# Two-layer decoder step: router products on column strips, the expert gather ahead of row numbers and weights, modulation pages moved, pages in pairs, pooling in parts

## The reference, cut to what matters

```
mod = silu(c) @ w_ada + b_ada            # 6 vectors of 1024: shift, scale, gate for mixer and for ffn
h = rms_norm(x, g_mix) * (1 + sc1) + sh1
q, k, v, u, g = split(h @ w_in)          # 4096 columns: 512, 512, 512, 512, 2 x 1024
o = differential attention(q, k, v)      # samples also read 256 cached keys and values each
y_pool = (trailing mean of u over 2/4/8/16 - u) @ w_pool
x = x + gt1 * ((g0 * (o @ w_branch[:512]) + g1 * (y_pool @ w_branch[512:])) @ w_out)
h2 = rms_norm(x, g_ffn) * (1 + sc2) + sh2
layer 0: f = (silu(h2 @ wg) * (h2 @ wu)) @ wd                       # dense, 2816 wide
layer 1: logits = h2 @ w_router; top 2 of 8 experts, softmax of the two
         f = sum over experts of weight * swiglu(h2, expert)        # each 3584 wide
x = x + gt2 * f
```

## Time and profile before

| what | value |
|---|---|
| median of 3 runs | 1683.52 us (1680.14 to 1684.52) |
| the profiled execution | 1683.85 us, span 1682.2 us |
| busy share of the span | PE 97%, PE weight load 61%, DVE 25%, ACT 9%, POOL 4% |
| DMA | 535.43 MB, mean 318 GB/s |
| chain that ended last | PE 80%, DMA 11%, DVE 4%, SP queue 3% |
| mean granted TensorE clock | 0.985 |

### The profile page before, as it was taken

The page is one execution under the profiler, slowest core; times in us unless marked ns, Lnnn a source line. Parts: engine busy times, 40 slices in busy tenths (PEclk is TensorE's granted clock), DMA queues, the critical chain, the costliest instruction groups (busy, mean ns, idle before and its releaser), DMA issues.

```text
span 1682.2 us, 35169 instructions
## 1 busy us (share of the span) xinstructions
PE 1624.7 (97%) x15778; PEld 1018.8 (61%) x15778; DVE 422.9 (25%) x966; ACT 158.4 (9%) x410; POOL 66.6 (4%) x114
## 2 busy tenths in 40 slices
PE   6999999999999989999999999999999999999997
PEld 3778887888886878882444444444445645445454
DVE  3368343101113784432101010101010101010114
ACT  2102301000002112130100000000000000000000
POOL 3101300000000010001000000000000000000100
PEclk8999999999999999988999999999999999999999
DMA  9999978564439987427999999999999999999995
GB/s 340 365 346 321 293 252 256 152 204 143 147 111 339 300 267 200 136 55 272 397 409 404 401 408 400 407 408 395 403 393 405 403 392 402 405 393 406 407 397 194
DMA packets 275562, 535.43 MB, mean 318 GB/s; under 512 B 17837, under 2 KB 167003, under 8 KB 262610
## 3 DMA queue, kind: packets, MB, share of 16 engines
q1 hardware_dynamic: 259920, 497.12, 81.5%
q0 software_dynamic: 8608, 28.65, 5.0%
q10 hardware_dynamic: 6882, 7.37, 1.4%
HBM read 517.70 MB, written 15.82 MB: 317 GB/s over the span
## 4 chain that ended last, share of the span: by engine, by line
PE 80%; DMA 11%; DVE 4%; SPq 3%; issue 1%; another core or an unknown queue 0%; ACT 0%; DVEq 0%
PE bank L1357 29%; PE bank L1377 13%; PE bank L1050 12%; PE bank L951 9%; PE bank L1247 5%; DMA ring<-in_w_exp_gate 4%; PE bank L1223 3%; DMA ring<-in_w_exp_up 3%; PE bank L1211 2%; PE bank L959 2%; SPq L573 1%; DMA area<-in_w_exp_down 1%; DMA ring<-in_w_ada 1%; DMA area<-q_rows 1%; SPq L590 1%
## 5 line engine op out<-in xcount | busy, mean ns | idle before, releaser
L1357 PE MATMUL bank<-ring,area 128*32 128x448 f32 x3072 | 294.6, 541 | 7.2 <-issue 3.9
L1357 PE MATMUL bank<-ring,xT 128*32 128x448 f32 x3072 | 294.5, 539 | 4.8 <-issue 3.0
L463 DVE TENSOR_TENSOR area<-bank,area 128x224 f32<-128x224 f32 x96 | 54.2, 564 | 787.4 <-ACT area L907 787.3
L1050 PE MATMUL bank<-hT,ring 128*128 128x264 f32 x1024 | 242.2, 392 | 2.2 <-ACT hT L744 2.2
L1357 PEld LDWEIGHTS bank<-ring,area 128*32 128x32 f32 x3072 | 115.6, 110 | 178.6 <-issue 163.8
L1357 PEld LDWEIGHTS bank<-ring,xT 128*32 128x32 f32 x3072 | 115.1, 110 | 176.2 <-issue 167.0
L1377 PE MATMUL bank<-area 128*32 128x256 f32 x3840 | 217.7, 379 | 3.2 <-issue 2.8
L1050 PEld LDWEIGHTS bank<-hT,ring 128*128 128x128 f32 x1024 | 194.4, 192 | 39.9 <-issue 6.7
L1377 PEld LDWEIGHTS bank<-area 128*32 128x32 f32 x3840 | 138.9, 110 | 75.0 <-issue 5.1
L951 PE MATMUL bank<-hT,ring 128*128 128x264 f32 x704 | 157.4, 386 | 0.0
L951 PEld LDWEIGHTS bank<-hT,ring 128*128 128x128 f32 x704 | 133.7, 190 | 23.2 <-issue 0.4
(11 more groups left out here) (296 smaller groups left out, 901.2 us busy)
## 6 DMA issues: line engine op xcount, KB each, us to landing
ring<-in_w_exp_gate SPq DMA_DIRECT2D x256, 448.0 KB, 14.4
ring<-in_w_exp_up SPq DMA_DIRECT2D x256, 448.0 KB, 14.9
area<-in_w_exp_down SPq DMA_DIRECT2D x64, 1024.0 KB
ring<-in_w_ada SPq DMA_DIRECT2D x96, 512.0 KB, 8.4
ring<-in_w_in SPq DMA_DIRECT2D x64, 512.0 KB, 9.3
ring<-in_w_exp_down SPq DMA_DIRECT2D x32, 1024.0 KB, 15.6
area<-in_w_exp_down SPq DMA_DIRECT2D x32, 512.0 KB
ring<-in_w_ff_gate SPq DMA_DIRECT2D x22, 512.0 KB, 6.9
```

Source lines behind the costliest of these rows:

```text
L463: dve.tensor_tensor(F["act_tok"][:, t, :].rearrange("p (i n) -> p n i", i=BODY), bank[t][:, SLICE:2 * SLICE].rearrange("p (n i) -> p n i", ...
L1050: mm = pe.matmul(bank[b][:, 0:T], w[:, c, :], hT[:, c, :], start=(c == 0), stop=(c == DC - 1))
L1357: mm = pe.matmul(bank[t][32 * g:32 * g + 32, 0:2 * SLICE].rearrange("p (s n) -> p s n", s=2), tokens[:, t, 32 * r:32 * r + 32], w[:, :, SL ...
```

## The change

- `later_ada` puts four modulation pages behind every second strip in place of two behind each. In layer 1 only pages 32 to 39 stay there; 40 to 47 go to the end of the stream, behind the output projection, and PE uses them in the router stage (40 to 43 ahead of the rank sums, 44 to 47 behind them). DVE reads them there (`read_mod(1, 7, 40, 47, ...)`, eight pages at a time).
- Strips of the input projection, of `w_branch` and of `w_out` are loaded two by two, one DMA of 1 MB with rows of 1 KB (`PAIRED`, `pair_cols`). SP waits until both slots are free, PE until the pair has landed.
- The sample values are used behind strips 27 and 29, four pages each.
- `pooling()` is split: the windowed sums and group 0 come behind `read_z(13)`, groups 1 to 3 behind `read_z(14)`, and both first `past_scores` behind `read_z(15)`.
- Router: `w_router` is the weight, padded to 32 columns; the eight chunks go to four column strips of PE in two rounds, `hT` moves (264 columns). DVE copies the four partial sums, and three products with a constant `fold` matrix add them and give tokens by experts. The transposes of `hT` stand around these products, chunk by chunk. ACT copies the x tokens between the norm's square root and its shift additions.
- Experts: DVE makes `got` first, then `most`, the modulation read and the three turns of gathered tiles; row numbers and weights follow. `gate_up_turn` waits tile by tile; the routing transposes behind turn 0 wait for a new semaphore `wt_ready`. The gather uses banks 3 to 5.
- Expert pages of turn 0 wait for pairs; the last six of the 16 now wait for modulation pages 40 to 45.
- The zeros tile is half as wide, and the 16 zero stores of layer 0 have rows of 1 KB.

```diff
         def later_ada(l, i):
-            first, last = ((16, 48), (32, 48))[l]
-            return range(first + 2 * i, min(first + 2 * i + 2, last))
+            first, last = ((16, 48), (32, 40))[l]
+            return range(first + 2 * (i - 1), min(first + 2 * (i + 1), last)) if i % 2 else range(0)
...
+            if l:
+                for n in range(40, 48):
+                    yield ada_page(l, n)
...
             for n, (key, src) in enumerate(stream):
+                if key[0] in PAIRED:
+                    if key[2] % 2 == 0:
+                        if n >= RING:
+                            sp.wait_ge(s.pages_used, freed(n + 1 - RING))
+                        sp.dma_start(pair_cols(n % RING), src).then_inc(page_in[n % RING], 16)
+                    continue
...
-                            sp.wait_ge(s.pages_used, STRAIGHT - RING + 2 * r + half + 1)
+                            sp.wait_ge(s.pages_used, STRAIGHT - RING + 2 * r + 2)
...
-                        pooling()
-                    if i >= 14:
-                        past_scores(i - 14)
+                    if i == 13:
+                        window_sums()
+                        pooled_minus_own(0)
+                    if i == 14:
+                        for g in range(1, H):
+                            pooled_minus_own(g)
+                    if i == 15:
+                        past_scores(0)
+                        past_scores(1)
...
+            def route(half):
+                for g in range(4):
+                    c = 4 * half + g
+                    mm = pe.matmul(bank[6][32 * g:32 * g + 32, 0:T], w_route[:, c, :], hT[:, c, :],
+                                   start=(half == 0), stop=(half == 1), skip_group_check=True)
+                if half:
+                    mm.then_inc(s.route_mm, 1)
+            pe.wait_ge(s.tok_out, 6)
+            for c in range(4):
+                pe.wait_ge(s.h_ready, DC * (2 * LAYERS - 1) + c + 1)
+                turn_h(c)
+            route(0)
+            pe.wait_ge(s.h_ready, DC * 2 * LAYERS)
+            route(1)
+            turn_h(4)
+            pe.wait_ge(s.logits_kept, 1)
             for i in range(3):
                 rows = min(P, T - i * P)
+                mm = pe.matmul(bank[6][0:rows, 272 + E * i:272 + E * i + E], FFN["wt_wide"][:, i * P:i * P + rows], const("fold"),
+                               start=True, stop=True)
+            mm.then_inc(s.route_mm, 1)
+            for c in range(5, DC):
+                turn_h(c)
+            for n in range(40, 44):
+                modulation(1, n, 7)
             pe.wait_ge(s.sel_ready, 1)
...
             mm.then_inc(s.rank_mm, 1)
-            pe.wait_ge(s.routed, 1)
-            pe.wait_ge(s.tok_out, 12)
+            for n in range(44, 48):
+                modulation(1, n, 7)
...
+            step(read_mod(1, 7, 40, 47, F["put"][:, 0, 0:S], 8))
+            for t in range(TILES):
+                dve.wait_ge(s.h_got_mm, t + 1)
+                dve.transpose(h_got[0][:, t, :], bank[3 + t][:, 0:S]).then_inc(s.h_got_out, 1)
```

More of the change, by code:

```diff
@@ L342, in build, with freed, experts @@
         landed, arrives = [0] * ERING, []
+        assert RING % 2 == 0
         for n, (key, _) in enumerate(stream):
-            landed[n % RING] += 16 * (PAGES if key[0] == "v" else 1)
-            arrives.append(landed[n % RING])
+            first = n - key[2] % 2 if key[0] in PAIRED else n
+            assert first % 2 == 0 or key[0] not in PAIRED
+            if first == n:
+                landed[n % RING] += 16 * (PAGES if key[0] == "v" else 1)
+            arrives.append((first % RING, landed[first % RING]))
         assert (STRAIGHT + 2 * DC) % 2 == 0
         eslot = [(STRAIGHT + i) % RING for i in range(RING)] + [RING + i for i in range(EXTRA)]
+        def freed(n):
+            return n + (2 if stream[n][0][0] in PAIRED and n % 2 == 0 else 1)
         def used_up(kind, l, i):
             return number[(kind, l, i)] + 1
-        def experts(dve, step, f, act_t, silu, add_f):
+        def experts(dve, step, f, act_t, silu, add_f, read_mod):
             F = FFN
@@ L421, in experts @@
             step(dve.tensor_tensor(key, F["two"], at(1).to_broadcast([P, 3, E]), ALU.mult))
[L422 to L427, removed]
+            dve.tensor_tensor(F["wt"], F["wt"], key, ALU.add).then_inc(s.wt_ready, 1)
             base = Step(dve, s.scaled)
@@ L740, in norm @@
                                scale=1.0 / D).then_inc(s.root_out, 1)
+                if n == 2 * LAYERS - 1:
+                    act.wait_ge(s.pooled, LAYERS)
+                    for i in range(3):
+                        rows = min(P, T - i * P)
+                        x = x_tok[:, i, :] if i < 2 else x_tok_s
+                        for half in range(2):
+                            act.wait_ge(s.tok_mm, 2 * i + half + 1)
+                            act.copy(x[:, 512 * half:512 * half + 512], bank[2 * i + half][0:rows, :]).then_inc(s.tok_out, 1)
                 shift = mod[:, 24 * (n % 2):24 * (n % 2) + 8, :]
@@ L856, in _ @@
                     touch(ACT.Exp)
[L857 to L867, removed]
+                    for half in range(2):
+                        act.wait_ge(s.tok_mm, 6 + half + 1)
+                        for i in range(3):
+                            rows = min(P, T - i * P)
                             act.copy(FFN["h_tok"][0:rows, i, :].rearrange("p (g r n) -> p r g n", g=4, r=DC)[:, 4 * half:4 * half + 4, :, :],
@@ L1269, in _, with turn_h @@
                     t.then_inc(s.tok_mm, 1)
[L1270 to L1271 removed]
+            def turn_h(c):
                 for i in range(3):
                     rows = min(P, T - i * P)
[L1274 to L1276 removed]
+                    tr = pe.transpose(bank[2 * i + c // 4][0:rows, (c % 4) * P:(c % 4 + 1) * P], hT[:, c, i * P:i * P + rows], ident)
+                if c % 4 == 3:
+                    tr.then_inc(s.tok_mm, 1)
```

149 lines of the change are left out of this document (82 added, 67 removed).

## The result

The kernel after takes **1659.16 us** (median of 4 runs, 1657.75 to 1660.88) against 1684.02 for the kernel before on the same chip (4 runs, 1680.14 to 1685.09): a ratio of 0.9858, 95% interval 0.9844 to 0.9872. It gains 24.9 us; 13.6 were forecast, and 1659.2 lies under the range's low end of 1661. The profiled execution took 1660.19 us, with a span of 1658.5 and a mean clock of 0.994 (0.985 before).

The account below looks back on a forecast made before the run. DMA was taken to bound the experts from turn 1's stream, PE nearly everything before the router. Terms -5.4 - 2.5 - 4.0 - 1.2 - 1.5 + 1 = -13.6 on 1683.85 gave 1670 us, range 1661 to 1681.

Parts of the forecast that it names:

- layer 0, pages in fours and waits: Layer 0 projection: modulation pages four in a run save 2.5 us, shorter waits at the value transposes 1.2 us.
- strips of layer 1: Layer 1 input projection: fewer modulation pages between the first and ninth strips, -5.4 us (bounds -3.5 to -5.6).
- queries, value transposes and the rest of layer 1's mixer: Layer 1: split pooling and earlier query fetch remove the first transposes' hole, 2.2 us wait left; -4.0 us.
- router stage up to gate-up: Router stage: earlier logits and a faster gather start gate-up at 763, -6.4 us.
- gate-up to the end: Experts: distance from gate-up's start to the end must grow by 5 to 7 us, or the forecast fails.
- the +1 for later turns: Experts: PE's lead ends sooner and the turns after it cost about 0.25 us more each, +1 us.
- The gather: Router stage: gather takes 5.2 us at full to 10.4 at half clock; gate-up between 760 and 769, taken as 763.
- Stores in the full stream: Experts: six indirect stores (2.16 MB) move from the idle stretch into the full DMA stream, +5.7 us.
- Rival 1: Experts: gate-up's earlier start counts in full, without the stores' cost or the later turns' cost; 1663, chance 0.15.
- Rival 2: Clock stays at 0.50 through the router stage and behind the second value transposes; 1677.8, chance 0.15.
- Rival 4: Strips: pairs land late and PE waits, 1.8 us for each of 12 pairs; 1692, chance 0.06.
- rival 3: Layer 1 projection: 1 KB rows no faster, queue stays full, the wait only moves; queries -0.3, 1674, chance 0.13.

Follow-up runs that it names:

- e8: Kernel before with only the pooling split in parts and both first past scores behind strip 15: 1682.40 us, ratio 0.9998.
- e6: Kernel after with the pooling whole again behind strip 12 and past scores behind strips 14 and 15: 1658.54 us, ratio 0.9853.
- e7: Kernel after with modulation pages 40 to 47 back in layer 1's projection, none in the router stage: 1667.35 us, ratio 0.9902.
- e5: Kernel after with every strip loaded singly again, 512-byte rows, instead of in pairs: 1660.76 us, ratio 0.9861.
- e12: e7 with 64 filler products that nobody reads in the router stage, in place of the pages: 1666.68 us, ratio 0.9900.
- e10: Kernel before with the six indirect stores held until the three gathered tiles are turned: 1684.62 us, ratio 0.9999.
- e2: Kernel after with the six indirect stores of token rows left out: 1654.58 us, ratio 0.9815.
- e3: Kernel after with the six indirect stores run twice: 1664.89 us, ratio 0.9880.
- e4: Kernel after with the row numbers computed ahead of the modulation read, so the stores start earlier: 1661.13 us, ratio 0.9854.
- e9: e4 with the six stores held until VectorE has turned the three gathered tiles: 1657.87 us, ratio 0.9848.

## Why the prediction was wrong, step by step

On the profiled executions the sum was -13.6 and -23.7 was measured. By the prediction's own steps:

| step | forecast | measured | from |
|---|---|---|---|
| layer 0, pages in fours and waits | -3.7 | -2.6 | first strip of layer 1, 520.52 to 517.90 |
| strips of layer 1 | -5.4 | -5.5 | 40.97 to 35.51 |
| queries, value transposes and the rest of layer 1's mixer | -4.0 | -6.5 | branch products 14.6 earlier, less the two above |
| router stage up to gate-up | -6.4 | -10.2 | gate-up 24.8 earlier, less 14.6 |
| gate-up to the end | +5.9 | +1.1 | 912.84 to 913.97 |

The last row's +5.9 is the stage's -1.5, less its -6.4, and the +1 for later turns. The sum missed by 10.1 us. Two steps failed: gate-up to the end by 4.8 and the router stage by 3.8. The queries add 2.5, and layer 0 takes back 1.1.

- **Strips and pages: right,** -5.5 for -5.4, and nothing else held the faster pace.
- **Queries: mechanism right, size too small.** The queue was empty and the fetch early. The wait left is 1.8 for my 2.2. Most of the difference is the clock, for which I had charged 1.5 us, half a chance of 3, and it did not fall: strip 17 took 5.26 us before by the timeline and takes 3.73 now. Another 0.6 lies behind the second transposes. What I put down to the pooling split is not its doing: alone it gives nothing (e8), and undone it costs nothing (e6). The emptier queue does it, and either way of emptying it is enough: by pairs (e7 has a store-to-fetch wait of 1.61 with the pages in place), or by the pages moved (e5 has 4.26, but its fetch lands in 7.0 us, against 9.1 before, and neither wait at the value transposes is over 1.87).
- **Router stage up to the gather: right.** The gather starts 4.0 us earlier against the last norm's sums; 3.8 were forecast at full clock (754.7 on 758.46).
- **The gather: the step that failed.** I placed gate-up at 763, between full and half clock, and the trace has the full end: 4.67 us from the gather's start to gate-up, against 10.90. That is 3.9 us of clock, which the eight pages keep up (e7, e12), and 2.3 us of waits, of which 1.8 is VectorE's late answer while GpSimd issued the stores. This second part I had not seen at all: I booked the stores behind the transposes as pure cost, while the old order cost 1.8 us too (e10). My "10.4 at half clock" stands in no row either: rows 8 have 8.60 us for the gather and 10.90 up to gate-up.
- **Stores in the full stream: right in kind, a little large.** 3.4 us by e2's trace, 4.9 and 5.4 by e2's and e3's medians, for 5.7.
- **Gate-up to the end: the step that I said the whole forecast stood on, and it did not come.** 5 to 7 us of growth were asked, 1.1 was found. Three things lie in it. Turn 1's stream follows gate-up by 2.5 us instead of 3.9, since turn 0 no longer begins at half clock: -1.4, of which I had booked -0.8. The stores: +3.4 for +5.7. And the +1 for a shorter lead has no counterpart: with the stores out of the stream page to end is 907.7 and 908.0 (e4, e2), a little less than before's 908.9. I charged the lost lead on top of the bytes, which counts one thing twice: in a DMA-bound stretch the end follows the stream's start and its bytes alone. Why before's is 0.9 to 1.2 us (0.1%) longer than these stays open.
- **Layer 0: 1.1 us short.** The wait at its second transposes is still 0.60 (0.69 before), and of the strips' saving a part is missing. Executions with the same layer 0 differ there by as much: from the first strip of layer 0 to that of layer 1 it took 475.0 us in e12, 476.5 in the kernel after and 476.7 in e9. This term is at the edge of what one trace can tell.

Rival 1 (gate-up's start counts in full, 1663) came nearest by its number, and not by its reason: the stores do cost 3.4 to 5 us. Rival 2 (clock low) is what e7 shows without the pages. Rival 4 did not occur: PE waits for no strip. The Trainium skill's 512-byte rule ("DMA: Bandwidth & Descriptors", Specifications), to which I had tied rival 3, is contradicted again, and the measurement decides. From 545 to 577 both the kernel before and e7 load strips with modulation pages between them: singles move 300 GB/s at a share of 1.10 (first window, before), pairs 350 GB/s at the same share (second window, e7).

```profile
545.00:577.00 32.00, 32.00 (x183) 25.15 (x176) 22.47 (x35) 5.84 (x13) 0.00 (x0) 1.00 1.10 300
```

```profile
545.00:577.00 32.00, 32.00 (x189) 25.84 (x182) 23.03 (x37) 5.20 (x11) 0.00 (x0) 1.00 1.10 350
```

## What to carry to other kernels

When DMA bounds the rest of the kernel, put the end down to two numbers only, when the stream starts and how many bytes follow; price every edit by those, and do not charge the loss of PE's lead as well. A small stage on narrow products between two dense ones can run at half clock: independent work of the same kernel moved into its gaps, if it fits them, pays twice, and filler that is longer than the gaps pays next to nothing. Ask of a moved block of DMA issues not only which bytes it now collides with, but which engine's wait it used to lie on.

## What the runs showed of the hardware

- While GpSimd issued six indirect stores (0.85 to 1.05 us each), VectorE's waits for TensorE were answered late: 5.5 us at the third tile in e4 and 1.8 us in the kernel before; with the stores held 0.07 us in e9 and in e10. Where all three tiles were ready before VectorE came to them, as in e8, the transposes ran back to back (1.11 us for three) while two store instructions ran, and small VectorE operations ran at their usual 0.18 us beside them. So it is not the execution that is held. The Trainium skill ("SBUF — State Buffer", SBUF: two separate sides) knows an exclusive port lock between VectorE and GpSimd, taken by VectorE's two-port modes or, against a GpSimd operation that reads SBUF, by VectorE operations with two SBUF inputs. It does not explain what is seen: the delayed operation has one input, from PSUM, and ran in its usual 0.45 us once it began. What delays the wait itself stays open.
- The clock of one and the same router stage, that of the kernel before, is 0.50 in the gather of one execution and 1.00 in another (8.60 us before, 4.77 in e8), worth some 4 us; e7's, without pages or fillers, was 0.50 in the profiled one. With the pages or the fillers ahead of the gather none of ten profiled executions showed the low level in the gather.
- 2.16 MB of indirect stores in the full stream cost 3.4 to 5.4 us, about what 2.16 MB at 405 GB/s (5.3 us) take.
